# A chunked delta rule: chunks of 128 tokens, the inverse's 32-blocks by substitution on another engine, two levels left, a new order of work

## What is computed

```
gc = cumsum(g)                       # log decay inside a chunk
decay = exp(gc_i - gc_j), j <= i
lmat = strictly lower part of (beta*k) k^T * decay
t_inv = (I + lmat)^-1                # triangular solve
u = t_inv (beta*v);   w = t_inv (beta*k*exp(gc))
a_qk = q k^T * decay
step over chunks:
    v_new = u_c - w_c S
    o_c   = (q*exp(gc)) S + a_c v_new
    S     = S * exp(gc_last) + (k*exp(gc_last - gc))^T v_new
```

## Time and profile before

| | us |
|---|---|
| median of 3 executions | 2775.07 |
| the profiled execution | 2776.59 |
| its span, first to last instruction | 2774.9 |
| TensorE busy | 2383.1 |
| VectorE busy | 1204.4 |
| ScalarE busy | 864.7 |
| GpSimd busy | 109.5 |
| delta stage, first to last TensorE work | 413.6 |

### The profile page before, as it was taken

How to read it: one execution, slowest core, us unless ns; L and a number is a source line. 1 busy time by engine, 2 the same in 40 slices (tenths; PEclk the granted TensorE clock), 3 DMA queues, 4 the chain that set the end, 5 groups by cost and what they waited for, 6 DMA issues and landing times. The chain is left out here.

```text
span 2774.9 us, 30417 instructions
## 1 busy us (share of the span) xinstructions
PE 2383.1 (86%) x11512; PEld 1876.5 (68%) x11512; DVE 1204.4 (43%) x2115; ACT 864.7 (31%) x1632; POOL 109.5 (4%) x109
## 2 busy tenths in 40 slices
PE   3978979999959779979999668969999995998676
PEld 3866667878848666768788555747777774786554
DVE  2458734324323687334233355653333433224353
ACT  2235523223222354333132243331222224125321
POOL 0000000000000000000000000001222220000000
PEclk9987889999979986999999879977889997999878
DMA  3320022323223200123323153210111113221110
GB/s 116 89 62 1 1 61 79 99 85 95 68 72 93 73 2 1 54 61 99 91 84 99 65 187 99 76 46 27 39 42 39 46 43 118 84 91 37 48 61 38
DMA packets 141962, 185.27 MB, mean 67 GB/s; under 512 B 7364, under 2 KB 105587, under 8 KB 141555
## 3 DMA queue, kind: packets, MB, share of 16 engines
q1 hardware_dynamic: 141810, 183.26, 20.9%
HBM read 173.27 MB, written 9.96 MB: 66 GB/s over the span
## 5 line engine op out<-in xcount | busy, mean ns | idle before, releaser
L153 DVE TENSOR_TENSOR weight_pairs<-weight_ring,weight_pairs 128x1024 fp32r<-128x1024 f32 (+2 forms) x313 | 379.7, 1215 | 629.0 <-ACT weight_pairs L144 628.1
L144 ACT ACTIVATE weight_pairs<-weight_ring 128x1024 fp32r<-128x1024 f32 (+2 forms) x313 | 326.4, 1045 | 807.3 <-PE psum L176 775.3
L174 PE MATMUL psum<-turned_x,weight_pairs 128*128 128x512 f32 (+1 forms) x704 | 296.0, 420 | 25.6 <-PEq L196 25.6
L176 PE MATMUL psum<-turned_x,weight_pairs 128*128 128x512 f32 (+1 forms) x704 | 285.0, 405 | 0.0
L175 PE MATMUL psum<-turned_x,weight_pairs 128*128 128x512 f32 (+1 forms) x704 | 284.2, 404 | 0.0
L174 PE MATMUL psum<-turned_x_mlp,weight_pairs 128*128 128x512 f32 x512 | 204.8, 400 | 12.8 <-PEq L196 12.8
L174 PE MATMUL psum<-weight_pairs,hidden 128*128 128x512 f32 x512 | 203.2, 397 | 0.0
L175 PE MATMUL psum<-turned_x_mlp,weight_pairs 128*128 128x512 f32 x512 | 202.7, 396 | 0.0
L176 PE MATMUL psum<-weight_pairs,hidden 128*128 128x512 f32 x512 | 202.0, 395 | 0.0
L175 PE MATMUL psum<-weight_pairs,hidden 128*128 128x512 f32 x512 | 201.8, 394 | 0.0
L176 PE MATMUL psum<-turned_x_mlp,weight_pairs 128*128 128x512 f32 x512 | 201.6, 394 | 0.0
(11 more groups left out here) (398 smaller groups left out, 3926.1 us busy)
## 6 DMA issues: line engine op xcount, KB each, us to landing
weight_ring<-in_w_in_dram SPq DMA_DIRECT2D x104, 512.0 KB, 3.5
weight_ring<-in_w_up_dram SPq DMA_DIRECT2D x64, 512.0 KB, 3.7
weight_ring<-in_w_down_dram SPq DMA_DIRECT2D x64, 512.0 KB, 3.7
weight_ring<-in_w_out_dram SPq DMA_DIRECT2D x24, 512.0 KB, 3.7
weight_ring<-in_ada_w_dram SPq DMA_DIRECT2D x24, 512.0 KB, 5.8
spilled<-v_t SPq DMA_DIRECT2D x22, 256.0 KB, 2.0
weight_ring<-in_w_proj_a_dram SPq DMA_DIRECT2D x8, 512.0 KB, 3.4
qk<-spilled SPq DMA_DIRECT2D x2, 2048.0 KB, 11.2
```

Source lines behind the costliest of these rows:

```text
L144: act.activation(self.pairs[:, i % SPLIT_RING, 0, 0:n], self.buf[:, i % RING, 0:n], ACT.Copy).then_inc(self.rounded, 1)
L153: dve.tensor_tensor(self.pairs[:, i % SPLIT_RING, 1, 0:n], self.buf[:, i % RING, 0:n], self.pairs[:, i % SPLIT_RING, 0, 0:n].bitcast(F32), ...
L174: pe.matmul(out, lhs[0], rhs[0], start=start, stop=False)
L176: return pe.matmul(out, lhs[1], rhs[0], start=False, stop=stop)
```

## The change

A chunk is now a whole tile of 128 tokens, so that the scan has 4 steps in place of 8 and no mask between two chunks. The inverse is made in two ways. Its 32 x 32 diagonal blocks (4 a head and tile, 32 for a tile's 8 heads) are solved by VectorE, all 32 at once, one on each of 32 partitions, by substitution: 31 pivots of an outer product and a subtraction, cut into 8 base steps of 4 pivots. To get a block on one partition, SP writes the lower triangle's diagonal blocks to DRAM (`out`) and loads them back as rows; the inverse and its transpose (turned by ScalarE) go back the same way into two DRAM images, which are loaded as `x_m` and `x_t` (`back`). TensorE keeps two levels (32 and 64), solve and scan. The exponents are split at the middle of a chunk, which needs one more column and four more short instructions in `normalize_and_spread`, and eight `scalar_tensor_tensor` of 64 columns in place of two wide instructions in form. beta is applied as ScalarE's scale in the copy of y. A dense step now has two products (six matmuls). The order is new; the base of the next tile stands beside the levels of the present one. The weight ring has 4 slots in place of 6, `onehot` is gone (a broadcast column of the identity takes its place) and only two masks are made.

The core of the diff:

```diff
-RING = 6
+RING = 4
 SPLIT_RING = 3
...
-            keep(decay_mask[:].rearrange("p (j w) -> p j w", w=CH), [[-CH, 2], [0, CH]], 0, 1, MASKED)
-            for i in range(LEVELS):
-                s = 1 << i
+            for i, s in enumerate(LEVELS):
...
+            own(dve.tensor_copy(split, exps[:, 0, :]))
+            own(dve.tensor_copy(lasts[:, 0:2 * T].unsqueeze(2),
+                                rows[:, 1, :].rearrange("p (n c) -> p n c", c=half)[:, :, half - 1:half]))
+
+            def part(ap, a):
+                return ap.rearrange("p (n a c) -> p n a c", a=2, c=half)[:, :, a, :]
+            first, second = lasts[:, 0:2 * T:2], lasts[:, 1:2 * T:2]
+            own(dve.tensor_tensor(part(split, 0), part(split, 0), spread(first, 2, half), ALU.subtract))
+            own(dve.tensor_tensor(part(exps[:, 0, :], 1), part(exps[:, 0, :], 1), spread(first, 2, half), ALU.add))
+            own(dve.tensor_copy(lasts[:, 3 * T:4 * T], first))
+            dve.tensor_tensor(lasts[:, 2 * T:3 * T], first, second, ALU.add).then_inc(lasts_ready, 1)
+            dve.tensor_tensor(exps[:, 1, :].rearrange("p (n c) -> p n c", c=CH), spread(second, 2, CH),
+                              split.rearrange("p (n c) -> p n c", c=CH), ALU.subtract).then_inc(lasts_ready, 1)
...
+SIZE = 32
+PROBLEMS = H * P // SIZE
+PIVOTS = SIZE - 1
...
+def delta_order():
+
+    lead = ("form dense form dense dense out dense dense base dense base dense base dense form dense base dense form "
+            "dense out base dense dense base dense base dense base dense back dense dense dense dense dense").split()
+    unit = "level dense base level dense level dense base level dense base level dense"
+    period = (unit + " " + unit + " read dense read base dense products dense products dense").split()
+    follow = "dense base back dense form dense form dense out".split()
+    names = {"read": "scan", "products": "scan"}
+    order = list(lead)
+    for t in range(T):
+        order += [s for s in period if s != "base" or t + 1 < T]
+        if t + 1 < T:
+            order += [s for s in follow if s not in ("form", "out") or t + 2 < T]
+    return [names.get(s, s) for s in order]
+
+
+BASE_STEPS = 8
...
         def _(sp):
+            def out():
+                for t in range(T):
+                    if t == 0:
+                        sp.dma_start(beta_rows[:], rows[:, 0, :]).then_inc(beta_out, 16)
+                        sp.wait_ge(blank, 2)
+                        sp.dma_start(image_m.rearrange("r h c -> r (h c)"), x_m).then_inc(images_out, 16)
+                        sp.dma_start(image_t.rearrange("r h c -> r (h c)"), x_t).then_inc(images_out, 16)
+                        sp.wait_ge(beta_out, 16)
+                        for b in range(NB):
+                            sp.dma_start(beta[b * NH:(b + 1) * NH], beta_rows.rearrange(
+                                "h (t b i) -> b h t i", t=T, b=NB)[b]).then_inc(beta_in, 16)
+                    else:
+                        sp.wait_ge(blocks_in, 16 * t)
+                    sp.wait_ge(lower_ready, G * (t + 1))
+                    for b in range(NB):
+                        sp.dma_start(block_rows[b].rearrange("h j i -> j h i"),
+                                     diagonal(lt[:, (t % 2) * NH * P:(t % 2 + 1) * NH * P], b)).then_inc(blocks_out, 16)
+                    sp.wait_ge(blocks_out, 16 * NB * (t + 1))
+                    if t:
+                        sp.wait_ge(inverted, t)
+                    sp.dma_start(blocks, block_rows.rearrange("b h j i -> (b h) (j i)")).then_inc(blocks_in, 16)
+                    yield
+
+            def back():
+                for t in range(T):
+                    sp.wait_ge(inverted, t + 1)
+                    if t == 0:
+                        sp.wait_ge(images_out, 32)
+                    else:
+                        sp.wait_ge(images_in, 32 * t)
+                    for b in range(NB):
+                        sp.dma_start(of_image(image_m, b), matrix(inverse)[b * NH:(b + 1) * NH]).then_inc(images_out, 16)
+                    sp.wait_ge(inverse_turned, t + 1)
+                    for b in range(NB):
+                        sp.dma_start(of_image(image_t, b), matrix(inverse_t)[b * NH:(b + 1) * NH]).then_inc(images_out, 16)
+                    sp.wait_ge(images_out, 32 + 2 * 16 * NB * (t + 1))
+                    sp.wait_ge(solved, G * t)
+                    sp.wait_ge(refined, 2 * G * t)
+                    sp.dma_start(x_m, image_m.rearrange("r h c -> r (h c)")).then_inc(images_in, 16)
+                    sp.dma_start(x_t, image_t.rearrange("r h c -> r (h c)")).then_inc(images_in, 16)
+                    yield
+
...
+            def dense():
+                for p in range(pairs):
+                    for m in range(KD):
+                        if m % (KD // 2) == 0:
+                            weights.send(sp, start + 2 * p + 2 * m // KD + 1)
+                        if m == 3 and p:
+                            spill(2 * p - 1)
+                        if m == KD - 1:
+                            spill(2 * p)
+                        yield
+                spill(2 * pairs - 1)
+
+            woven(order, out=out(), back=back(), dense=dense())
...
         def _(pe):
+            def form():
...
+                        pe.matmul(psum[:, 0, column(hh)], ident[0:NH, h:h + 1].broadcast_to([NH, P]), rows[:, 1, tile],
+                                  start=True, stop=True)
+                    for hh in range(HG):
+                        h = HG * g + hh
+                        pe.matmul(psum[:, 1, column(hh)], k_t[:, h, tile], k_t[:, h, tile], start=True, stop=True)
+                        mm = pe.matmul(psum[:, 2, column(hh)], k_t[:, h, tile], q_t[:, h, tile], start=True, stop=True)
                     mm.then_inc(formed, 1)
                     yield
...
+            def level():
+                for i in range(N):
+                    t, g = i // G, i % G
...
+                    for lv in range(2):
+                        j = 2 * i + lv
                         pe.wait_ge(level_ready, j + 1)
                         if lv == 0:
-                            pe.wait_ge(inverse_ready, i + 1)
+                            pe.wait_ge(images_in, 32 * (t + 1))
+                            pe.wait_ge(attn_ready, formed_before)
+                            pe.wait_ge(exp_ready, formed_before)
+                            pe.wait_ge(stored, i)
...
-                            pe.wait_ge(x_refined, i * (ML - 1) + lv)
+                            pe.wait_ge(x_refined, i + 1)
...
+                            c = slice(at + hh * P, at + (hh + 1) * P)
+                            if lv == 0:
+                                pe.matmul(psum[:, 1, column(hh)], x_t[:, c], y[:, column(hh)], start=True, stop=True)
+                            mm = pe.matmul(psum[:, 2, column(hh)], y[:, column(hh)], x_t[:, c], start=True, stop=True)
                         mm.then_inc(z_done, 1)
                         yield
...
         def _(act):
+                    act.activation(heads(eg)[:, :, 0:P // 2], heads(psum[:, 0, :])[:, :, 0:P // 2], ACT.Exp)
+                    for hh in range(HG):
+                        part = slice(hh * P + P // 2, (hh + 1) * P)
+                        growth = act.activation(eg[:, part], psum[:, 0, part], ACT.Exp,
+                                                bias=last_decay[:, HG * g + hh, T + t:T + t + 1])
+                    growth.then_inc(exp_ready, 1)
                     yield
...
+
+            def base():
+                for t in range(T):
+                    for step in range(BASE_STEPS):
+                        if step == BASE_STEPS - 1:
+                            act.wait_ge(inverted, t + 1)
+                            if t:
+                                act.wait_ge(images_out, 32 + 2 * 16 * NB * t)
+                            act.activation(matrix(inverse_t), matrix(inverse).rearrange("p r c -> p c r"),
+                                           ACT.Copy).then_inc(inverse_turned, 1)
...
+                        for hh in range(HG):
+                            h = HG * g + hh
+                            copy = act.activation(y[:, column(hh)], psum[:, 0, column(hh)], ACT.Copy,
+                                                  scale=tok_cols[:, 0, t, h:h + 1])
+                        copy.then_inc(y_copied, 1)
                         yield
...
         def _(dve):
-            def prepare():
+            dve.memset(x_m, 0.0).then_inc(blank, 1)
+            dve.memset(x_t, 0.0).then_inc(blank, 1)
+
+            def form():
...
+                    for hh in range(HG):
+                        h = HG * g + hh
+                        for a, col in ((0, 1), (1, 4)):
+                            part = slice(hh * P + a * P // 2, hh * P + (a + 1) * P // 2)
+                            arg = dve.scalar_tensor_tensor(out=dec[:, part], in0=psum[:, 0, part],
```

(72 more changed lines are left out.)

424 lines of the change are left out of this document (201 added, 223 removed).

## The result

The changed kernel takes 2673.73 us (median of 4 runs, 2673.19 to 2687.88), the kernel before, run beside it, 2780.59 us (4 runs, 2773.88 to 2793.44). The ratio is 0.9629, 95% interval 0.9587 to 0.9671: faster, and inside the predicted range. The sum was made against one profiled execution. The profiled execution of after took 2687.88 us against 2776.6 of before: 88.7 us less, where 88.6 were forecast. That the two agree to 0.1 us is chance: this execution is the longest of the four, the other three took 2673 to 2674 us, and by the medians the gain is some 103 us (0.0371 x 2776.6). Only one execution of a run has a profile, so which part was shorter in the other three is not shown.

A forecast was written before the change was run, and what follows sets the result against it. The delta stage was taken as bound by TensorE before, and after by a chain through VectorE and DRAM trips: 84 + 45 + 140 + 58.5 + 2.5 = 330 us; 2776.6 - 83.6 - 5 = 2688 us, range 2615 to 2745.

The forecast's parts named there:

- TensorE's part: Delta stage: 448 products and all turns go, leaving 232 us of TensorE work at full clock.
- VectorE's part: Delta stage: new substitution work of 26 us a tile, 104 in all; together with units, low halves and collisions 220 us.
- Collisions: Delta stage: VectorE instructions wait for GpSimd's to end; 3.3 us a unit, 26 us in all.
- The trips: Delta stage, each tile, through DRAM: images' way back 12.5 us (scattered writes 7 of it), blocks out and in 7.4 us.
- The beginning: Delta stage before the first tile: forms, DRAM trip, base steps and way back, 84 us with 41 us of TensorE work.
- Outside the stage: Rest of the kernel: start -4.2 us, masks -4.9, normalization +2, weight ring +2; sum -5 us.
- the ring of four: Modulation stage: fewer weight slots may make it wait, between 0 and 8 us; 2 us taken.
- What would show it: Expected profile signs: PE busy near 240 us of 330, base-row means near 0.35 us, a TensorE idle stretch over 20 us.
- (c): Rival, image and block transfers: scattered 128-byte runs cost double the mean packet, 12 us more a tile, 2736 us; chance 0.15.
- (a): Rival, delta stage: TensorE stays the bound, VectorE's steps fit the gaps and DRAM trips are hidden, 2598 us; chance 0.10.
- (b): Rival, VectorE's substitution: each short row costs a start of its own; at 50 ns a row 2886 us, slower; chance 0.05.
- (d): Rival, delta stage: order less out of step, GpSimd meets few base steps, middle tiles take TensorE's 52 us, 2632; chance 0.20.

The follow-up runs named there:

- run 3: Changed kernel with one of three matmuls of each dense product in the delta stage left out (176 matmuls): 2675.56 us; delta stage 325.3 us, -3.9.
- run 2: Changed kernel with every second pivot of VectorE's substitution left out: 2648.1 us; delta stage 296.9 us, -32.3.
- run 9: Changed kernel reordered, four base steps a unit instead of three, the images' trip beside the scan: 2692.17 us; delta stage 334.3 us, +5.1.
- run 12: Changed kernel with thirty of 31 pivots a tile left out, all trips, levels and waits kept: 2640.66 us; delta stage 282.5 us, -46.7.
- run 4: Changed kernel with six of eight scattered image writes a tile left out, both loads kept: 2679.38 us; delta stage 323.5 us, -5.7.
- run 10: Changed kernel with the first image on its own semaphores, loaded once its four writes landed: 2670.6 us; delta stage 324.0 us, -5.2.
- run 7: Changed kernel with GpSimd's products of the delta stage on one of four heads, except the first unit's level matrices: 2666.69 us; stage 318.8 us, -10.4.
- run 1: Kernel before with a weight ring of 4 slots in place of 6, nothing else: 2780.8 us, ratio 1.0002; modulation stage 65.6 us, +6.3.
- run 8: Kernel before with the third of three matmuls of each dense product left out in the delta stage: 2772.48 us; stage 408.1 us, -11.3.

## Why the prediction was right

The forecast mechanism held: the chain through VectorE's steps and two trips through DRAM sets the stage, and TensorE has slack. TensorE's slack is shown by run 3, VectorE's place on the path by runs 2, 9 and 12, the images' way back in the first and the last tile by runs 4 and 10. In the two tiles between the prediction had the path through the forms, the blocks' trip and the first base step to the second level, with the images' way back beside it, and that is how it came out: 32 us from the end of the products to the second level were forecast, and it was 29.8 us in tile 1 and 31.7 in tile 2. It has no term for GpSimd on this way, for which TensorE stands 4.7 us in each of the two. Its size held too (-90.2 us where -83.6 were forecast), though the whole sum fits better than its parts. By the prediction's own milestones, from the stage's first instruction:

| milestone | predicted | measured |
|---|---|---|
| last base step of tile 0 | 71.5 | 63.9 |
| last base step of tile 1 | 133.7 | 126.7 |
| the same, tile 2 (a tile of 70) | 203.7 | 198.8 |
| the same, tile 3 | 273.7 | 272.8 |
| last store | 330 | 323.9 |

(Predicted: 84 less the way back of 12.5; then 84 + 45, and 4.7 from a tile's products to its base step.)

- **TensorE's part.** 232 us at full clock were forecast; it was busy for 255 us at a mean granted clock of 0.88. The first stretch has 0.76, and the clock came back to 0.93 only from tile 1 on. The 2.5 us for the lower clock were not tested.
- **VectorE's part.** Elements and starts were right: 62 instructions x 0.19 and 10,912 x 1.04 ns gave 23.1 us a tile, 92.4 in four; run 7, with few collisions left, shows 86.4 + 8.5 of gaps = 94.9. Collisions were over-priced: 26 us against the 15 that VectorE's busy time lost in run 7 (186.7 to 171.8), in which a few collisions are left. The 64-column pieces went the other way, 0.28 us each and not 0.21.
- **The trips.** Blocks 5.2 us (7.4), way back 11 (12.5). The scattered writes were taken at 7 us, between 1.8 and 10.1. In tile 1 the first four go out beside ScalarE's turn, and from the issue of the other four at 2026.94 to the loads at 2030.44 it is 3.5 us, near the lower end. The turn and the loads took more than their terms: 2.1 and 5.4 us, not 1.1 and 4.4. The first return took longer, 15 us from the last pivot at 1962.05 to the landing at 1977.1, since four other transfers stood ahead in SyncE's queue and its eight issues took 5.8 us instead of 3.3. ScalarE's turn of 1,024 elements by a strided read has no row before.
- **The beginning** was 7.6 us too long in the sum, the two middle tiles 2 and 4 us too short, and the last one 5 us too long; they make up for each other in part, so 330 is nearer to 323.9 than its parts are. That is luck in part.
- **Outside the stage.** -5 in the sum; the four rows of the table give -1.5, and the rest of the program +3.0, where 0 was forecast. The step that was mis-sized is the ring of four: "between 0 and 8 us, I take 2" against 6.3 in run 1. Items land in 4.8 us now (5.8 before), yet two fewer are under way. The normalization stretch grew by 3.6 us, not 2. 1.6 of them lie before its first copy of turned rows (line 1578 before, 1581 after), where the four short instructions stand; the others lie behind, and no run takes them apart. The masks gave 6.0 us and not 4.9.
- **What would show it.** The base rows' means are 0.40 and 0.41, not 0.35: they carry the collisions. TensorE's longest idle stretch was 12.9 us and not over 20, and it stands behind ScalarE's turn; dense steps follow, and then 5.2 us directly before the first level. The sign of (c) was near: VectorE was idle for 9.0, 6.8, 7.5 and 9.7 us before the images landed in the four tiles, under the 10 named.

The rivals: (a) falls with run 3. (b) falls with the timeline: 31 rows of one element take as long as one row of 31. (c) falls with the queue's own times and with run 4. Three quarters of 2,048 runs x 65 ns / 16 engines are 6.2 us and would be 12.5 at double the price; without them the way back was shorter by 2.6 us in tile 0 and 1.7 in tile 3, where it is on the path. Of the Trainium skill's rule (DMA: Bandwidth & Descriptors, Specifications) that a transfer under 512 B is read, modified and written, these runs show no price worth a term: a write of 32 KB in runs of 128 B landed 1.6 us after its issue (the blocks' writes, median of 16). (d) has the wrong place: GpSimd met fewer base steps than priced, but the tiles of 72 and 74 us never came near 52, and in run 12, almost without substitution, they still took 64.

One reading of before needs mending: "the stage is as long as TensorE's work in it". That is so, but run 8 shows that work taken from TensorE alone would have given back little. That the change paid since it took away three levels' chain of product, copy and subtraction together with TensorE's time fits this, but no run takes the levels out one by one.

Stays open: how much of the first part is due to ScalarE's queue (the wait of 12.9 us), which no run changed, what an earlier mask product on GpSimd would give in tiles 1 and 2, and what a second buffer for the inverse would allow. No version tried is shown to beat the changed kernel; the tenth run's stage is 5 us shorter, inside the scatter of its whole time.

## What to carry to other kernels

An engine busy for 99% of a stage tells that nothing else is longer, not how much its work is worth: look for the chain behind it before pricing a cut by its busy time (here 11 of 40 us). Moving a serial, fine-grained part to a second engine paid here, where it also took the three levels' rounds between engines out of the stage; what it costs is its own chain, and here two thirds of the first half was on the path and a quarter of the second. Before a trip is hidden, see tile by tile whether anything waits for it: two of the reorderings here were made against a wait that only the first and the last tile have. A prefetch depth that is enough where weights are used slowly must be priced in the stage that uses them fastest.
